# Latent attention: inverse row sums applied to the probabilities, or to the finished outputs

## What is computed

```python
s = (einsum('bhqd,bkhd->bhqk', qn, k_nope) + einsum('bhqr,bkr->bhqk', qr, k_rope)) * scale
s = where(key_idx[None, :] <= q_idx[:, None], s, -inf)
pr = softmax(s, axis=-1)
return einsum('bhqk,bkhd->bqhd', pr, v)
```

## Time and profile before

| what | value |
|---|---|
| median of three runs | 1994.52 us |
| the profiled execution, its own time | 1991.63 us |
| its span in the trace | 1989.8 us |
| TensorE matmul busy | 1934.5 us (97%) |
| VectorE busy | 1100.2 us (55%) |
| ScalarE busy | 832.7 us (42%) |
| GpSimd busy | 41.7 us (2%) |
| granted TensorE clock, mean | 0.998 of full speed |
| attention loop, layer 0 | 151.72 to 192.14 us |
| attention loop, layer 1 | 818.83 to 859.27 us |

### The profile page before, as it was taken

How to read it: one execution, slowest core, us unless ns; L and a number is a source line. 1 busy time by engine, 2 the same in 40 slices (tenths; PEclk the granted TensorE clock), 3 DMA queues, 4 the chain that set the end, 5 groups by cost and what they waited for, 6 DMA issues and landing times.

```text
span 1989.8 us, 28365 instructions
## 1 busy us (share of the span) xinstructions
PE 1934.5 (97%) x12070; PEld 1562.4 (79%) x12070; DVE 1100.2 (55%) x1585; ACT 832.7 (42%) x1206; POOL 41.7 (2%) x34
## 2 busy tenths in 40 slices
PE   7999899999999999998999999999999999999998
PEld 6875678888888888657788888887787777799887
DVE  6567846543444544876644334457676674443474
ACT  5257534322223313773432222245554653335273
POOL 0100000000000000000000000000000000020000
PEclk9999999999999999999999999999999999999999
DMA  6240003322322323201132233233212222212102
GB/s 236 94 125 1 24 24 106 106 80 101 106 99 73 114 88 111 63 1 46 64 106 93 84 109 106 73 108 127 101 69 106 85 74 96 100 63 95 64 16 81
DMA packets 28268, 170.01 MB, mean 85 GB/s; under 512 B 3632, under 2 KB 3888, under 8 KB 12912
## 3 DMA queue, kind: packets, MB, share of 16 engines
q1 hardware_dynamic: 28144, 168.21, 24.4%
HBM read 161.77 MB, written 2.10 MB: 82 GB/s over the span
## 4 chain that ended last, share of the span: by engine, by line
PE 88%; DVE 7%; ACT 3%; issue 1%; DMA 0%; SPq 0%; DVEq 0%; ACTq 0%
PE accumulators L705 26%; PE accumulators L707 25%; PE accumulators L706 25%; PE accumulators L731 4%; DVE ring_low L2142 1%; ACT arena L1652 1%; PE accumulators L845 1%; DVE accumulators L2400 1%; ACT ring_high L1555 1%; DVE arena L2413 1%; DVE arena L2463 1%; PE accumulators L1420 1%; PE accumulators L1439 1%; PE accumulators L953 1%; PE accumulators L987 1%
## 5 line engine op out<-in xcount | busy, mean ns | idle before, releaser
L705 PE MATMUL accumulators<-arena_split,ring_high 128*128 128x512 f32 (+1 forms) x2212 | 864.4, 391 | 18.2 <-DVE ring_low L2254 10.4
L706 PE MATMUL accumulators<-arena_split,ring_high 128*128 128x512 f32 (+1 forms) x2212 | 852.4, 385 | 0.0
L707 PE MATMUL accumulators<-arena_split,ring_low 128*128 128x512 f32 (+1 forms) x2212 | 852.4, 385 | 0.0
L705 PEld LDWEIGHTS accumulators<-arena_split,ring_high 128*128 128x128 f32 x2212 | 416.7, 188 | 110.6 <-DVE ring_low L2254 10.4
L706 PEld LDWEIGHTS accumulators<-arena_split,ring_high 128*128 128x128 f32 x2212 | 416.8, 188 | 86.0 <-issue 4.8
L707 PEld LDWEIGHTS accumulators<-arena_split,ring_low 128*128 128x128 f32 x2212 | 416.7, 188 | 83.5
L1555 ACT ACTIVATE ring_high<-ring 128x2048 fp32r<-128x2048 f32 (+3 forms) x161 | 281.5, 1749 | 405.5 <-PE accumulators L707 403.6
L2142 DVE TENSOR_TENSOR ring_low<-ring,ring_high 128x2048 fp32r<-128x2048 f32 (+3 forms) x161 | 336.9, 2093 | 185.5 <-ACT ring_high L1555 184.8
L1573 ACT ACTIVATE arena<-accumulators 128x512 f32<-128x512 f32 x72 | 43.1, 598 | 277.2 <-DVE accumulators L2123 277.1
L2123 DVE TENSOR_TENSOR accumulators<-accumulators,rstd 128x512 f32<-128x512 f32 x72 | 50.3, 699 | 118.8 <-PE accumulators L707 118.8
L2622 DVE TENSOR_TENSOR arena<-arena,accumulators 128x512 f32<-128x512 f32 x44 | 30.3, 688 | 119.6 <-PE accumulators L707 118.1
(11 more groups left out here) (362 smaller groups left out, 1722.0 us busy)
## 6 DMA issues: line engine op xcount, KB each, us to landing
ring<-slabs_in SPq DMA_DIRECT2D x115, 1024.0 KB, 4.8
ring<-slabs_in SPq DMA_DIRECT2D x38, 704.0 KB, 4.0
ring<-slabs_in SPq DMA_DIRECT2D x4, 576.0 KB, 3.5
h<-x_in SPq DMA_DIRECT2D x4, 512.0 KB, 7.6
con<-con_in SPq DMA_DIRECT2D x1, 2048.0 KB, 9.3
arena<-arena SPq DMA_DIRECT2D x8, 256.0 KB, 4.1
arena<-arena SPq DMA_DIRECT2D x32, 64.0 KB, 2.5
out<-arena SPq DMA_DIRECT2D x8, 256.0 KB, 2.0
```

Of the source, the lines that this page charges most:

```text
L705: pe.matmul(out, weight[0], right[0], start=start, stop=False)
L706: pe.matmul(out, weight[0], right[1], start=False, stop=False)
L707: return pe.matmul(out, weight[1], right[0], start=False, stop=stop)
```

## The change

The probabilities are no longer scaled. For each pair of heads VectorE takes one reciprocal of the pair's 8 columns of row sums, each repeated over 64 columns, into `A(4 + pair)`: 128x512 results (at u = 9, 17, 25 and 33). TensorE transposes this tile in four blocks into a bank (`spread_factors`, behind the transposes of unit u - 3 at u = 12, 20, 28 and behind the loop), so that the inverse sums lie along the tokens, once for each of the 128 output rows. ScalarE copies the bank back to `A(4 + pair)`. The outputs of a pair are no longer copied by ScalarE: VectorE multiplies them with the factors as they leave their bank (`scaled_values`, at u = 18, 26 and 34; the last pair between the two halves of the retention scores). The transposes now wait for the exponential itself. Copies of 384-wide transposed probabilities move from ScalarE to VectorE. ScalarE waits for the last product before it splits `A(4)` and `A(5)`. A semaphore `sums_inverted` takes the place of `rows_scaled`.

```diff
--- before.py
+++ after.py
@@ -612,7 +612,7 @@
             return f"out{l}_0"
 
         TOKENS = (slice(0, T // 2), slice(T // 2, T))
-        T_OWNER = ("dve", "act", "act", "act")
+        T_OWNER = ("dve", "act", "dve", "act")
         P_TILES = 6
         VALUE_UNITS = {0: (0,), 2: (1,), 4: (2, 3)}
 
@@ -845,8 +845,17 @@
                             mm = pe.matmul(b[64 * e:64 * e + 64, j * P:T], A(39 + j)[:, 0, hd * 64:(hd + 1) * 64],
                                            turned(l, hd)[:, j, j * P:T], start=(j == 0), stop=(j == NT - 1))
                     if blocks[-1] == NT - 1:
-                        enter(key, "act")
+                        enter(key, "dve")
                         mm.then_inc(psum_ready, 1)
+
+                def spread_factors(pair_of):
+
+                    pe.wait_ge(sums_inverted, cnt.next(sums_inverted))
+                    b = group(("factor", l, pair_of), "act")
+                    for j in range(NT):
+                        js = slice(j * P, (j + 1) * P)
+                        mm = pe.transpose(b[:, js], A(4 + pair_of)[:, 0, js], cst("ident"))
+                    mm.then_inc(psum_ready, 1)
 
                 for u in range(len(units) + 3):
                     if u == 3:
@@ -860,7 +869,7 @@
                              [k96[0:MLA_QK, hd, 0:(i + 1) * P]], N=(i + 1) * P)
                     if 0 <= u - 3 < len(units):
                         w = u - 3
-                        pe.wait_ge(rows_scaled, cnt.next(rows_scaled))
+                        pe.wait_ge(*taken(("s", l, w)))
                         b = group(("t", l, w), T_OWNER[w % NT])
                         for j in range(units[w][1] + 1):
                             js = slice(j * P, (j + 1) * P)
@@ -868,6 +877,9 @@
                         mm.then_inc(psum_ready, 1)
                     if u >= 13 and (u - 13) % 8 in VALUE_UNITS:
                         attended((u - 13) // 8, VALUE_UNITS[(u - 13) % 8])
+                    if u >= 12 and u % 8 == 4 and u < len(units):
+                        spread_factors((u - 12) // 8)
+                spread_factors(MLA_H // 2 - 1)
                 if l:
                     gemm(("vlow", l), "act", slice(0, 32), [small[:, V1 + 32 * k:V1 + 32 * (k + 1)] for k in range(2)],
                          [A(14 + k)[:, 0, :] for k in range(2)])
@@ -1688,9 +1700,8 @@
                         f(turned(l, w // NT)[:, 0:i + 1, i * P:(i + 1) * P],
                           bank(("t", l, w))[:, 0:(i + 1) * P].rearrange("p (j t) -> p j t", t=P),
                           ACT.Copy).then_inc(cnt.up(act_released), 1)
-                    last = 14 + max(VALUE_UNITS)
-                    if u >= last and (u - last) % 8 == 0 and (u - last) // 8 < MLA_H // 2 - 1:
-                        copy_out(("pv", l, (u - last) // 8), A(4 + (u - last) // 8)[:, 0, :])
+                    if u >= 13 and u % 8 == 5 and u < MLA_H * NT:
+                        copy_out(("factor", l, (u - 13) // 8), A(4 + (u - 13) // 8)[:, 0, :])
                     if u < MLA_H * NT:
                         act.wait_ge(psum_ready, finished(("s", l, u)))
                         act.wait_ge(bias_ready, cnt.next(bias_ready))
@@ -1699,6 +1710,7 @@
                         f(probabilities(u), bank(("s", l, u))[:, 0:(u % NT + 1) * P], ACT.Exp, bias=stat[:, 1, u:u + 1],
                           scale=-1.0, accum_out=stat[:, 2, u:u + 1]).then_inc(cnt.up(act_released), 1)
 
+                copy_out(("factor", l, MLA_H // 2 - 1), A(3 + MLA_H // 2)[:, 0, :])
                 if l:
                     copy_out(("vlow", l), A(2)[0:32, 0, :], rows=slice(0, 32))
                 for hp in range(2):
@@ -1716,8 +1728,6 @@
                         b = bank(("vgate", l, hp))
                         f(A(hp)[:, 0, :], b[:, :], ACT.Sigmoid, bias=pr(f"v0{l}", hp)).then_inc(cnt.up(act_released), 1)
                     act.preload_act_table_set(ROOTS)
-                copy_out(("pv", l, MLA_H // 2 - 1), A(3 + MLA_H // 2)[:, 0, :])
-
 
                 for hp in range(2):
                     act.wait_ge(psum_ready, finished(("ry", l, hp)))
@@ -1754,6 +1764,7 @@
                     if n == 2:
                         prepare(f"out{l}_0", 1)
                     if n == 3:
+                        act.wait_ge(*taken(("pv", l, MLA_H // 2 - 1)))
                         for k in MIX_ORDER[0:2]:
                             high(MIX_HIGH[k], A(k)[:, 0, :])
                     if n == len(LEVELS) - 2:
@@ -2391,6 +2402,13 @@
                     dve.wait_ge(cnt.sem, cnt.value)
                     tt(A(25, 2), A(27, 2), A(25, 2), SUB).then_inc(cnt.up(decay_summed), 1)
 
+                def scaled_values(pair_of):
+
+                    dve.wait_ge(psum_ready, finished(("pv", l, pair_of)))
+                    dve.wait_ge(*taken(("factor", l, pair_of)))
+                    y = A(4 + pair_of)[:, 0, :]
+                    tt(y, bank(("pv", l, pair_of))[:, :], y, MUL).then_inc(cnt.up(dve_released), 1)
+
                 between = {2 * NT: lambda: decay_scan(0), 4 * NT: lambda: decay_scan(1), 6 * NT: decay_before}
                 for u in range(MLA_H * NT + 4):
                     if u < MLA_H * NT:
@@ -2405,12 +2423,13 @@
                         dve.wait_ge(psum_ready, finished(("t", l, w)))
                         cp(turned(l, w // NT)[:, 0:i + 1, i * P:(i + 1) * P],
                            bank(("t", l, w))[:, 0:(i + 1) * P].rearrange("p (j t) -> p j t", t=P)).then_inc(cnt.up(dve_released), 1)
-                    w = u - 1
-                    if 0 <= w < MLA_H * NT:
-                        dve.wait_ge(*taken(("s", l, w)))
-                        dve.reciprocal(stat[:, 3, w:w + 1], stat[:, 2, w:w + 1]).then_inc(cnt.up(dve_done), 1)
-                        dve.wait_ge(cnt.sem, cnt.value)
-                        ts(probabilities(w), probabilities(w), stat[:, 3, w:w + 1], None, MUL).then_inc(cnt.up(rows_scaled), 1)
+                    if u >= 18 and u % 8 == 2 and (u - 18) // 8 < MLA_H // 2 - 1:
+                        scaled_values((u - 18) // 8)
+                    if u >= 9 and u % 8 == 1:
+                        dve.wait_ge(*taken(("s", l, u - 2)))
+                        factors = A(4 + (u - 9) // 8)[:, 0, :].rearrange("p (j e c) -> p e j c", j=NT, e=2)
+                        sums = stat[:, 2, u - 9:u - 1].rearrange("p (e j) -> p e j", j=NT)[:, :, :, None]
+                        dve.reciprocal(factors, sums.broadcast_to((P, 2, NT, 64))).then_inc(cnt.up(sums_inverted), 1)
                     if u in between:
                         between[u]()
 
@@ -2463,6 +2482,7 @@
                             tt(dst, b[:, 0:n], con[:, o + hd * T:o + hd * T + n], MUL).then_inc(cnt.up(dve_released), 1)
                         off += n
                     if hp == 0:
+                        scaled_values(MLA_H // 2 - 1)
                         removal_key()
                 keys()
                 decayed()
```

More of the change, by code:

```diff
@@ L458, in two_blocks @@
         bias_ready = sem("bias_ready")
-        rows_scaled = sem("rows_scaled")
+        sums_inverted = sem("sums_inverted")
         ret_rope_ready = sem("ret_rope_ready")
```

## The result

The changed kernel takes 2015.88 us (median of 4 runs, 2012.24 to 2019.26); the kernel before, timed beside it, 1994.72 (1991.6 to 1996.45). The ratio is 1.0109, 95% interval 1.009 to 1.0129: slower, by 21 us where 14.6 were forecast. The profiled execution took 2014.96 with a span of 2013.2, 23.4 more than the span before. By its stretches: layer 0's loop +8.2, layer 1's loop +8.05, layer 0's tail +1.8, layer 1's tail +7.0, all the rest -1.7 (a tail here runs from t to the removal key's follower, L2431 before and L2450 after: to its start in layer 0, to its end in layer 1).

A forecast was written before the change was run, and what follows sets the result against it. TensorE carries 88% of the chain, but VectorE's work nearly fills each pair of heads. Two loops at +5.0, layer 0's tail +1.0 and +1.05, layer 1's +2.5: +14.6 us on 1994.5, forecast 2009.0 us, range 1993 to 2018.

The forecast's parts named there:

- t: End of the last exponential in a layer's attention loop, from which the tail's times are counted.
- R: Time of one VectorE reciprocal with 512 results a partition, in the attention loops: taken as 3.4 us, ends 0.49 and 5.5.
- Rivals 1 and 2: Loops: reciprocal streams, R near 0.5, 1989 us (chance 0.12); in between, R near 2 or more overlap, 1994 us (0.12).
- rival 4: Loops: a dearer reciprocal, 4.5 us, 8 instructions x 1.1 more, +23.4 us, 2018; chance 0.15.
- The banks: Loops: transposes of inverse sums and next score wait for banks VectorE frees behind the reciprocal; later intervals 11.75, 12.5, 12.9 us.
- Rival 3: Loops: load only, reciprocal 3.4 us but bank waits made up, 0.5 each later interval; +6.5, 2001 us; chance 0.10.
- E: End of the wide reciprocal on VectorE, 5.7 us after the pair's bank reduction starts; no exponential from 8j+2 on before it.
- The first interval: Each loop's u 0 to 8, no wide reciprocal, TensorE and ScalarE bound it: 8.3 us for 8.85, -0.55.
- TensorE has work for about 4 us of that, then stands: Loops: during the 5.7 us to the reciprocal's end, TensorE works about 4 us, then stands at the inverse sums' transposes.
- Layer 0's tail: After layer 0's loop: key-square products later, +1.0 us, and last product ahead of the removal key, +1.05 us.
- Layer 1: ... +2.5: Layer 1's tail: value product vlow, formerly under cover, ends behind the factor transposes at t+5.9 for t+3.45: +2.5 us.
- Costed at nothing: ScalarE's changed copies and its new wait, and sixteen transposes a layer in TensorE's waiting time (1.8 us if uncovered).

The follow-up runs named there:

- the halves: Changed kernel with each 512-wide reciprocal split into two of 256 columns, each behind four sums: 1992.77 us, ratio 0.9993.
- the clock held up: Changed kernel with two 512-wide matmuls that nobody reads ahead of the transposes at u = 12, 20 and 28: 2010.09 us, ratio 1.0081.
- the narrow version: Changed kernel with a pair's 8 sums inverted once (128x8) and spread to 512 columns by a copy: 1983.93 us, ratio 0.9947.

## Why the prediction was right or wrong

**R, right.** Taken 3.4, measured 3.35. The slope between a 128x1 and a 128x16, 6.2 ns an element, held over 512, and 1.75 us for 256 lies on the same line. Rivals 1 and 2, below 1.5 and near 2, fall with it, and rival 4's 4.5. The Trainium skill ("VectorE: DVE Perf Modes", "First, the fixed hardware budget") gives reciprocal a repeat count of 8. The prediction's estimate from that page was 4.3 us; the measured 3.35 decides against it.

**The banks, right.** Rival 3, load only, is refuted by the halves: with the same load the interval is 10.75, against 12.34 for the whole reciprocal at clock 1.00; and with the copies on ScalarE the transposes start at E+0.06. E+1.07 and E+1.58 stand in the timeline for E+1.15 and E+1.9, and with the clock held up the three intervals sum to 36.99 where 37.15 was worked out.

**The first interval, mis-sized.** I kept TensorE and ScalarE at the work that the earlier trace rows showed and took 8.3; it was 7.08. The same 37 products of TensorE count as 7.92 busy us before and as 7.08 after, so a busy time read in a stretch with waits was no lower bound; why it shrank, no run here shows. That is 1.2 us a layer in the change's favour.

**"TensorE has work for about 4 us of that, then stands": the step that failed.** I priced the stand at its own length, with TensorE at full clock behind it. Behind each of the loops' six stands of 1.9 to 2.1 us TensorE's clock went to its lower level for 3.4 us: 9.0 us in all. With -2.4 from the first intervals and -0.3 from the later ones, the loops' +10 became +16.3.

**Layer 0's tail, right.** +2.05 predicted, +1.8 measured; kks at t+4.02 for t+4.05. Timeline of VectorE, kernel after, with the product between the two halves of retention as described:

```profile
200.08 3.35 DVE L2432 RECIPROCAL arena<-stat 128x512 f32<-128x512 f32 x1 [0.75 <-ACT arena L1710]
...
212.05 0.69 DVE L2410 TENSOR_TENSOR arena<-accumulators,arena 128x512 f32<-128x512 f32 x1 [1.83 <-PE accumulators L845]
212.66 1.41 DVE L2443 SCALAR_TENSOR_TENSOR arena<-arena,par 128x512 f32<-128x512 f32 x2
```

**"Layer 1: ... +2.5", mis-sized: it was +7.0.** The path was right: kks stood at t+5.95 for t+5.9. Then came two things that I had not counted. Timelines of layer 1's tail, kernel after, TensorE, VectorE and GpSimd:

```profile
882.09 1.98 PE L731 MATMUL accumulators<-arena,con 128*128 128x512 f32 x4
...
887.40 0.48 PE L731 MATMUL accumulators<-arena 64*128 64x128 f32 x2 [0.98 <-DVE arena L2482]
887.82 2.78 PE L731 MATMUL accumulators<-arena,small 32*128 32x512 f32 x4
890.53 1.11 PE L845 MATMUL accumulators<-ring_high_plain,arena 128*64 128x512 f32 x1
```
```profile
895.11 0.69 DVE L2410 TENSOR_TENSOR arena<-accumulators,arena 128x512 f32<-128x512 f32 x1 [6.67 <-PE accumulators L845]
895.72 3.36 DVE L2443 SCALAR_TENSOR_TENSOR arena<-arena,par 128x512 f32<-128x512 f32 x2
```
```profile
898.34 0.74 DVE L2443 SCALAR_TENSOR_TENSOR arena<-arena,par 128x512 f32<-128x512 f32 x1
```
```profile
895.52 2.35 POOL L3002 TENSOR_TENSOR arena<-arena 128x1024 f32<-128x1024 f32 x1
```

(The line at 898.34 is the second of the removal key's two steps by itself.) First, from 888.9 to 895.7 TensorE is at the lower clock again: the four 32-row products take 2.78 us for 1.98, the value product's widest 1.11 for 0.61. This time it is behind a stand of only 0.98 us; the 2.1 us stand at 877.6, in the same tail, had brought no fall. From kks to the value product's end 12.97 us pass; in layer 0, with 1.98 for these four products added, it would be 10.0, so 3.0 are clock. Second, the last product waits for that end, and the removal key behind it now runs beside GpSimd's product: 3.36 us for 1.41, of which its first step takes 2.7 and its second the usual 0.74. The step that had met it before, L2431 at 1.82, now takes 0.53. That leaves 0.7, and the last product another 0.6 that I had called free. 2.5 + 3.0 + 0.7 + 0.6 = 6.8 of the 7.0. The trace agrees here with the Trainium skill ("SBUF — State Buffer", "SBUF: two separate sides"), by which VectorE with two SBUF inputs and a reading GpSimd share a port pair: whichever starts first holds it for its whole instruction, and the other waits. GpSimd's product starts 0.2 us ahead of the removal key's first step, and that step ends some 0.5 us behind the product's end at 897.87.

**Costed at nothing, right:** ScalarE and SP are no more of the chain than before; in the loop of the change the four transposes of a pair are through at 178.57, when the product has just freed the next score's bank (178.51). Where TensorE no longer stands, in the narrow version, they are uncovered, as the prediction had it: 0.44 for four.

**The range** (1993 to 2018) held the time; 2016 lies above the forecast's own 2004 to 2014, near rival 4's 2018 for another cause than that rival's. That it came so near is partly luck: against the forecast's +14.6 the profile has +9.0 of clock in the loops and +4.5 in layer 1's tail, and -2.7 in the loops, -0.2 in layer 0's tail and -1.7 elsewhere, which no run explains.

**Open:** what decides whether the clock falls behind a stand. The same stand was followed by a fall in one layer and not in the other, stands of 2.1 us in both tails of the change by none, one of 0.98 us by a fall of 6.8 us, and kernels whose loops were kept at 1.00 lost part of it again in other stretches. The four runs of the change order by their mean clock (2012.24 at 0.992, 2014.96 at 0.991, 2016.80 at 0.990, 2019.26 at 0.989), which may be why a gain of a few us in a loop doesn't always reach the median.

## What to carry to other kernels

Price a reciprocal by the results it writes, not by the distinct values in it: invert on the narrow tile and spread with a copy afterwards (0.20 + 0.43 us for 3.35). For other costly elementwise operations the same question is worth asking; no run here answers it. On an engine that works in order, look at the longest instruction beside the load: ask which banks wait for what stands behind it, and whether TensorE has enough queued to cover it; here two halves at different places left the time at that of before, where the whole put it 21 us above. Where TensorE is made to stand for about 2 us in a busy stretch, add to the stand what it may lose afterwards at its lower clock: here 1.4 to 1.6 us each time in the change, and once 2.8.

## What was not expected of the hardware

- A reciprocal's time is linear in its results: 0.16 us for 1, 0.20 for 8, 0.25 for 16, 1.75 for 256, 3.35 for 512; reading the same 8 sums 64 times over makes it no cheaper, since 512 results lie on the line through 1 and 16 separate values. A copy that spreads the same 8 values over 512 columns takes 0.43.
- TensorE's granted clock went to 0.50 behind all six stands of 1.9 to 2.1 us in the loops of the change, at most 1.5 us after TensorE had begun again, and stayed there for 3.4 us though TensorE was busy nearly all that time. In another run the same kind of stand was followed by 6.8 us of it in one layer and by none in the other.
- A 128x512 step of VectorE with two SBUF inputs that started 0.2 us after a 128x1024 product of GpSimd took 2.7 us for 0.75; it ended 0.5 us after the product.
